# Index scores inside the query tiles, two ranking steps behind every search round, and attention outputs normalised per tile

## The reference, cut to what matters

```
h = rms_norm(x); q, k, v, qi, ki, wi, xp = split(h @ w_in)       # rotary on q, k, qi, ki
prompt:  sc[q, key] = sum_h wi[q, h] * relu(qi[q, h] . ki[key])    # 8 index heads, causal
         sel = top_k(sc, 128);  o = softmax(q.k over sel) @ v      # 8 heads, 2 kv heads
sample:  the same over 2048 cached keys in pages: 256 are selected, their k and v rows gathered
pool:    m = (window mean(xp) - xp) @ w_pool * scale
x = x + rms_norm([o, m] @ w_out)
x = x + rms_norm((gelu(conv(h2 @ w_gate)) * (h2 @ w_val)) @ w_down)
```

## Time and profile before

| what | value |
|---|---|
| three runs | 1585.71, 1589.93 (median), 1590.79 us |
| profiled execution | 1585.85 us, of which the span is 1584.1 us |
| busy in the span | PE 1435.0, weight loads 1239.6, DVE 803.7, ACT 432.3, POOL 184.1 us |
| granted clock over the span | 0.932 of 2.4 GHz |

### The profile page before, as it was taken

How to read it: one execution, slowest core, us unless ns; L and a number is a source line. 1 busy time by engine, 2 the same in 40 slices (tenths; PEclk the granted TensorE clock), 3 DMA queues, 4 the chain that set the end, 5 groups by cost and what they waited for, 6 DMA issues and landing times. The chain is left out here.

```text
span 1584.1 us, 25392 instructions
## 1 busy us (share of the span) xinstructions
PE 1435.0 (91%) x9676; PEld 1239.6 (78%) x9676; DVE 803.7 (51%) x1752; ACT 432.3 (27%) x761; POOL 184.1 (12%) x200
## 2 busy tenths in 40 slices
PE   4999957998899999999988988599979999999995
PEld 2765643687899999999957547356969999999995
DVE  1127777434665656712142486863366565665221
ACT  3111113534322222422131120254342222224220
POOL 1000354002100000000040005430030000000002
PEclk8999976898999999999979999587989999999997
DMA  8870112002122222222159402020212222222321
GB/s 322 176 103 27 34 36 77 5 28 80 67 93 89 85 91 93 86 97 88 69 215 172 87 1 70 1 81 1 80 41 94 93 87 87 91 103 74 111 76 54
DMA packets 46316, 133.17 MB, mean 84 GB/s; under 512 B 6319, under 2 KB 25615, under 8 KB 38911
## 3 DMA queue, kind: packets, MB, share of 16 engines
q1 hardware_dynamic: 43423, 119.52, 25.2%
q0 software_dynamic: 2816, 12.62, 2.3%
HBM read 119.94 MB, written 12.82 MB: 84 GB/s over the span
## 5 line engine op out<-in xcount | busy, mean ns | idle before, releaser
L779 PE MATMUL ps<-moR_r,W_r 128*128 128x260 f32 x1408 | 285.4, 284 | 0.0
L779 PEld LDWEIGHTS ps<-moR_r,W_r 128*128 128x128 f32 x1408 | 218.1, 190 | 0.0
L779 PE MATMUL ps<-hT_r,QZC_r 128*128 128x260 f32 x896 | 183.4, 286 | 0.0
L779 PE MATMUL ps<-moR_r,QZC_r 128*128 128x260 f32 x704 | 146.5, 289 | 12.3 <-DVE hT_r L1822 12.1
L779 PE MATMUL ps<-moR_r,SQ_r 128*128 128x260 f32 x704 | 142.1, 283 | 0.0
L779 PEld LDWEIGHTS ps<-hT_r,QZC_r 128*128 128x128 f32 x896 | 141.3, 193 | 0.0
L779 PE MATMUL ps<-hT_r,SQ_r 128*128 128x260 f32 x704 | 140.6, 281 | 0.0
L766 PE MATMUL ps<-hT,W 128*128 128x260 f32 x576 | 132.8, 388 | 0.0
L779 PEld LDWEIGHTS ps<-moR_r,QZC_r 128*128 128x128 f32 x704 | 110.6, 192 | 16.0 <-issue 8.6
L766 PEld LDWEIGHTS ps<-hT,W 128*128 128x128 f32 x576 | 109.4, 192 | 17.1 <-issue 0.6
L1864 DVE TENSOR_TENSOR SEL<-ps,rstd 128x520 f32<-128x520 f32 x44 | 30.8, 700 | 154.3 <-PE ps L779 149.4
(11 more groups left out here) (318 smaller groups left out, 2728.0 us busy)
## 6 DMA issues: line engine op xcount, KB each, us to landing
W<-in_w_gates SPq DMA_DIRECT2D x44, 512.0 KB, 3.2
W<-in_w_vals SPq DMA_DIRECT2D x44, 512.0 KB, 3.2
W<-in_w_downs SPq DMA_DIRECT2D x16, 1408.0 KB, 6.0
W<-in_w_pairs SPq DMA_DIRECT2D x12, 1024.0 KB, 7.5
pages_by_slot<-moR SPq DMA_DIRECT2D x8, 1024.0 KB, 5.4
yR<-pages_by_slot SPq DMA_DIRECT2D x16, 512.0 KB, 17.9
W<-in_w_outs SPq DMA_DIRECT2D x8, 1024.0 KB, 4.9
W<-in_w_kv SPq DMA_DIRECT2D x2, 1312.0 KB, 10.3
```

Of the source, the lines that this page charges most:

```text
L779: last = mm(ps[:, 2 * (g % 2) + f, 0:HT], w(k), x(k)[:, f * HT:(f + 1) * HT], start=(k == 0 and n == 0), stop=(k == nk - 1 and n == 2))
```

## The change

Dots are taken in the order of head pairs and put into the products of QI_T+2, QI_T+3, XP_T and XP_T+1, six each, behind the steps named in `at`; DVE adds them between its rotary steps. Ranking of tile 1 and the search come after all of them. Each of the 20 search steps is followed by `rank(2)`, the nineteenth by three more, and the rest of the ranking is spread over attention steps 3 to 23. In attention the probabilities are no longer scaled. `values` takes the transposed probabilities as weights (128 columns) and moves 64 columns of v, so that outputs have queries on partitions; per tile DVE scales them at once (`outputs_normed`), PE turns them back in four transposes, ACT copies them. `keys_turned` moves from steps 21 to 24 to steps 17 to 20, `pick_d` from 6 to 5, `pick_e` from 9 to 7, `pool_tiles` from 14 to 24, where its evacuation moves from ACT to DVE.

```diff
-SCORED = 10
-ROPES = {16: (4,), 18: (5,), 19: (6,)}
+DOTS = [(t, h) for j in range(4) for t in (1, 2, 3) for h in (2 * j, 2 * j + 1)]
+ROPES = {12: (4,), 15: (5,), 17: (6,)}
 # PE
+                def dot(d):
+                    def go():
+                        t, h = DOTS[d]
+                        if d == 0:
+                            pe.wait_ge(*kt_ev(l, 4))
+                        if d % 6 == 0:
+                            wait_alone(pe, *rope_done(l, d // 6 + 1))
+                        if d >= 2:
+                            wait_alone(pe, *dot_relu(l, d - 1))
...
-                    tile8(QI_T + j, 1 + j // 2, j % 2)
+                    tile8(QI_T + j, 1 + j // 2, j % 2, extras=dots, at=range(2, KD) if j >= 2 else ())
...
+                steps = [scores_by_page] + [count(s) for s in range(COUNTS)] + [pick_a, pick_b, pick_c]
+                page_products()
+                arrived(l, 4)
+                for j in (2, 3):
+                    pe.wait_ge(*evac(l, XP_T + j - 1))
+                    tile8(XP_T + j, 4, j % 2, extras=steps, at=(1, 4, 7) if j == 2 else (1, 3, 5, 7))
...
-                    wait_alone(pe, *list_ev(l, 1))
-                    pe.wait_ge(*o_ev(l, 1))
+                    wait_alone(pe, *ss_ready(l, 1))
+                    pe.wait_ge(*qs_ev(l, 2))
+                    pe.wait_ge(*o_ev(l, 2))
...
-                picks = {6: pick_d, 14: pool_tiles, 26: sample_scores, 28: scores_by_row, 33: sample_probs_turned,
-                         34: sample_values}
-                picks.update({21 + q: (lambda q=q: keys_turned(q)) for q in range(4)})
+                def outputs_turned(t):
+                    wait_alone(pe, *o_normed(l, t + 1))
+                    for j in range(4):
+                        last = turn(ps[:, 6 + t % 2, j * P:(j + 1) * P], ON[:, j * P:(j + 1) * P], ident)
+                    last.then_inc(o_turned.sem, 1)
+                picks = {5: pick_d, 21: sample_scores, 23: scores_by_row, 24: pool_tiles, 28: sample_probs_turned,
+                         30: sample_values}
+                picks.update({17 + q: (lambda q=q: keys_turned(q)) for q in range(4)})
+                turned = {8 * t + 12: t for t in range(NT - 1)}
...
-                    pe.wait_ge(*prob_ready(l, i + 1))
+                    pe.wait_ge(*exp_done(l, i + 1))
...
-                        last = mm(ps[64 * n:64 * n + 64, 6 + t % 2, j * P:(j + 1) * P],
-                                  NAT[:, kt, 200 + 64 * n:264 + 64 * n], ART[:, i % 2, kt * P:(kt + 1) * P],
+                        last = mm(ps[:, 6 + t % 2, 64 * p:64 * p + 64], ART[:, i % 2, kt * P:(kt + 1) * P],
+                                  NAT[:, kt, 200 + 64 * n:264 + 64 * n], start=(kt == 0), stop=(kt == t))
 # DVE
-                for j in range(4):
-                    rope(j)
+                for ropes, first in (((0,), 0), ((1,), 6), ((2, 3), 12)):
+                    for j in ropes:
+                        rope(j)
+                    for d in range(first, first + 6):
+                        add_dots(d)
...
-                    d = SCORED + 1 + n
-                    if d < 24:
-                        add_dots(d)
-                        rank(1 if d >= 16 else 0)
-                    else:
-                        rank(2)
+                    rank(2)
                     for j in ROPES.get(n, ()):
                         rope(j)
-                rank(4)
-                rope(7)
+                    if n == 18:
+                        rank(3)
+                        rope(7)
...
+                def outputs_normed(t):
+                    dve.wait_ge(*pv_mm(l, N_HEADS * (t + 1)))
+                    if t:
+                        dve.wait_ge(*o_turned(l, t))
+                    nc.vector.reciprocal(sums[:, t % 2, :], sums[:, t % 2, :]).then_inc(o_recip.sem, 1)
...
-                    if 4 <= i < 2 * N_HEADS:
-                        rank(-(-len(ranks) // (2 * N_HEADS - i)))
+                    if 3 <= i < 24:
+                        rank(-(-len(ranks) // (24 - i)))
```

More of the change, by code:

```diff
@@ L416, in build @@
         pms_mm = Signal("pms_mm", 1)
+        pm_ev = Signal("pm_ev", 4)
         pms_ev = Signal("pms_ev", 1)
@@ L758, in arrived, with product @@
                 pe.wait_ge(*w_in_slot[c % 2](l, 16 * dmas_before(c)))
-            def product(g, lhsT, rhs, nk, extras=None, before=None):
+            def product(g, lhsT, rhs, nk, extras=None, at=(), before=None):
                 for k in range(nk):
@@ L821, in partner @@
                     last.then_inc(rot_mm.sem, 1)
+                def dot(d):
[7 more added lines that the diff above has]
+                            wait_alone(pe, *dot_relu(l, d - 1))
+                        rows = slice(64 * (h % 2), 64 * (h % 2) + 64)
+                        mm(ps[:, 4 + d % 2, 0:P * (t + 1)], qiT[rows, h // 2, t * P:(t + 1) * P],
+                           kiT[rows, 0:P * (t + 1)], start=True, stop=True).then_inc(dot_mm.sem, 1)
+                    return go
+                dots = [dot(d) for d in range(24)]
                 for j in range(4):
@@ L844, in layer @@
                 partner(3)
+                arrived(l, 3)
+                pe.wait_ge(*evac(l, XP_T - 1))
+                tile8(XP_T, 3, 0, extras=dots, at=range(2, KD))
                 pe.wait_ge(*rope_done(l, 4))
@@ L850, in layer @@
                 mm(ps[:, 7, 0:8], const("ofrow", 8), WI[0:8, 4, :], start=True, stop=True).then_inc(qib_mm.sem, 1)
-                arrived(l, 3)
-                pe.wait_ge(*evac(l, XP_T - 1))
-                tile8(XP_T, 3, 0)
+                pe.wait_ge(*evac(l, XP_T))
+                tile8(XP_T + 1, 3, 1, extras=dots, at=range(1, KD - 1))
                 pe.wait_ge(*qib_ev(l, 4))
@@ L938, in layer @@
                     pe.wait_ge(*evac(l, Q_T + j - 1))
-                    tile8(Q_T + j, 5 + j // 2, j % 2, extras=counts)
+                    tile8(Q_T + j, 5 + j // 2, j % 2, extras=steps, at=(1, 4, 7))
                     if j >= 1:
@@ L1057, in layer @@
                         picks[i]()
+                    elif steps:
+                        steps.pop(0)()
+                    if i in turned:
+                        outputs_turned(turned[i])
                     if 2 <= i < UNITS + 2:
@@ L1219, in layer, with relu @@
                 copy(kT[:, SEQ:TOK], ps[:, 7, 8:8 + NB]).then_inc(kt_ev.sem, 1)
-                q_copy(2, QI_T + 2)
-                q_copy(3, QI_T + 3)
+                def relu(d):
+                    t, h = DOTS[d]
+                    n = P * (t + 1)
+                    act.wait_ge(*dot_mm(l, d + 1))
+                    if d >= 4:
+                        act.wait_ge(*dot_acc(l, d - 3))
+                    nc.scalar.activation(RB[:, d % 4, 0:n], ps[:, 4 + d % 2, 0:n], ACT.Relu).then_inc(dot_relu.sem, 1)
+                for j in range(2):
+                    for d in range(6 * j, 6 * j + 6):
+                        relu(d)
+                    q_copy(2 + j, QI_T + 2 + j)
+                for d in range(12, 18):
+                    relu(d)
                 def xp_copy(j):
@@ L1281, in exponentials @@
                         act.wait_ge(*pt_mm(l, i - 3))
[L1282 to L1284 removed]
+                    t, p = divmod(i, N_HEADS)
+                    nc.scalar.activation(ARP[i % 4][:, 0:n], ARS[:, i % 2, 0:n], ACT.Exp, bias=att[:, i % 4:i % 4 + 1], scale=-1.0,
+                                         accum_out=sums[:, t % 2, p:p + 1]).then_inc(exp_done.sem, 1)
                 def probs_copied(i):
@@ L1582, in layer @@
                 ts(spread, const("spread"), wcol[:, 8:9], None, ALU.mult).then_inc(w_spread.sem, 2)
+                for d in range(18, 24):
+                    add_dots(d)
                 dve.wait_ge(*sdot_mm(l, 1))
@@ L1587, in layer @@
                 nc.vector.tensor_reduce(snew[:, :], sdot[:, :], AX.X, ALU.add).then_inc(snew_ready.sem, 1)
-                for d in range(8):
-                    add_dots(d)
                 for r in range(TOPK_P // 8):
```

210 lines of the change are left out of this document (90 added, 120 removed).

## The result

The changed kernel takes 1638.16 us (median of 4 runs, 1637.46 to 1641.43) against 1590.36 before: ratio 1.031, 95% interval 1.029 to 1.034. It is slower, as forecast, but by 48 us and not by 26, and 1638 lies 5 us above the range. The profiled execution took 1641.43 us, 55.6 more than that of before.

A forecast was written before the change was run, and what follows sets the result against it. It saw a path through DVE's ranking, search, attention and list, then POOL's gather, then PE. Keys at 1050.4 plus 70.9, less 0.8, made 14 us a layer, 28 in all: 1614, stated as 1616, range 1592 to 1633.

The forecast's parts named there:

- Page products: Dots moved ahead of the page products in layer 1: 17.5 us later, page products at 910.6.
- search: Search behind the ranking of tile 1: starts at 930, takes 72.0 us, rounds of 3.18 set by DVE.
- attention start: Attention starts on DVE at 1002 in place of 990.05, 12 us late.
- list: First attention steps with one-hot rows take 12.2 us; the list is ready at 1021.8, 3 us earlier than before.
- The gather: Keys land at 1050.4, 28.6 us after the list; PE reaches step 17 near 1042 and waits 8 us.
- hidden after all: Rival: PE reaches step 17 later or the list comes 12 us earlier, so no gather wait; 1588, chance 0.10.
- the faster one: Rival: ranking hides in DVE's wait for PE's count during search, saving up to 21 us; 1580, chance 0.07.
- The tail: PE work from the keys at step 17 to the output projection: 60.4 us, plus the slow-clock allowance.
- 10.5 for the slow clock: Tail allowance: 1.5 behind the gather wait, 7 behind the sample scores, 2 behind the sample values.
- the slow clock holds: Rival: PE stays at 0.50 from the keys through the pool tiles, 6 us a layer more; 1626, chance 0.14.
- the 0.8: Taken off the projection's start at 1121.3, as its first matmuls may find the full clock.
- The value matmuls: Turned value matmuls in attention, 64 moving and 128 weight columns: priced by weight load, 0.21 for two passes, no gain.

The follow-up runs named there:

- pool14: The changed kernel with the pool tiles moved back from attention step 24 to step 14: 1647.9 us.
- late_rows: The changed kernel with pool tiles at step 14 and gathered-row work at the old steps (keys 21, sample scores 26, sample values 34): 1604.3 us.
- late_wide: late_rows with most value matmuls moving their 64 columns of v twice (128 columns): 1585.3 us.
- after_wide: The changed kernel with most value matmuls moving their 64 columns of v twice and nothing else: 1626.7 us.
- straight_early: The changed kernel with the old kernel's value matmuls, scaling and output copies, gathered keys still at step 17: 1632.6 us.
- after_dense: The changed kernel plus unread 128 x 512 matmuls, six before the wait for gathered rows and four before the row scores: 1626.1 us.
- late_dense: late_rows plus four unread 128 x 512 matmuls ahead of the row scores: 1611.7 us.
- late_one: late_rows with one ranking action per search round in place of two: 1612.0 us (1597.5 to 1621.1).

## Why the prediction was wrong in size

- **Page products, search, attention start, list** (17.5, 72.0, 12.2): held within 2.5 us. The 2 us come from the dots' stretch (page products 912.7). There the third rotary step cost 1.7 and not 1.0, the wait for the new score 0.65 and not 0.4, and the rotation product at 879.25 ran at the slow clock, 1.86 us to the next row where before had 0.96. The search's 72.0 measured 72.1 (960.18 to 1032.29).
- **The gather:** the wait appeared, in both layers, at the first key transpose, 5.6 for 8, because PE reached step 17 at 1047.3 and not 1042, at the slow clock already. The "hidden after all" rival (0.10) is out, and so is the faster one.
- **The tail, 60.4 and 10.5 for the slow clock: here is the step that failed.** The mechanism was named, the price was wrong. 77.6 was measured in layer 1 and 80.7 in layer 0, so with my 60.4 the clock costs 17.2 and 20.3. I took 10.5 from the old kernel, where the clock returned 13 us after the sample scores, and assumed it would return as soon in the new one. It came back for good only behind the pool tiles. With full-clock steps of 2.48 us in tile 3 (1134.76 to 1137.24) instead of my 2.66, 60.4 was if anything too much, and 17.2 too little. The wait for the rows was priced as a wait. pool14 and late_rows, 44 us apart, show that using the rows early costs far more than the wait's 3 to 6 us, since the clock is down at the keys and stays down.
- **The rival "the slow clock holds" (0.14, 6 a layer)** happened and was too cheap: 6.7 more in the tail of layer 1, and the 0.8 that I had taken off for the projection's first matmuls did not come. PE's slow way to step 17 cost nothing, it only shortened the wait. I had priced the rival for the keys to the pool tiles alone; the 17 us from the sample values to the projection ran at 0.50 too.
- **The value matmuls:** "no gain" was nearly right for their price: four products of tile 3 take 0.94 at the full clock against 1.01 before (1093.63 to 1094.64 in PE's timeline), and 0.99 with 128 moved columns in late_wide (1079.83 to 1080.82). But I weighed only what a product costs at a given clock and not what it does to the clock. late_wide shows that, on the kernel with the late rows: 1604.3 became 1585.3.
- **Behind the projection's start** I had zero; 3.9 and 3.4 us came, from where the clock fell in the feed-forward part. Other kernels of this study scatter as much there with the same instructions, so as far as the runs show this part is luck, bad luck here.
- **The sum** for layer 1 in the profiled execution: keys 2.5, tail 6.7, projection 0.8, behind it 3.4, so 13.4 beyond the forecast of 14. Twice 27.4 is 54.8, and 55.6 was measured.

A product of two passes with 128 weight and 64 moving columns takes 0.235 us here at the full clock and 0.433 at the half one (1.73 for four). The Trainium skill (TensorE: Matmul & The Clock Gate, LDWEIGHTS) gives a weight load as its columns over 1.2 GHz, 0.107 us for 128; the estimate from it for the two passes is 0.21, as in the prediction. The trace agrees at the full clock, within 0.03; at 0.50 it does not, the product takes twice that. So the rule was sound for the sum at the full clock and did not cover the half of the tail that ran at the other.

What stays open: what keeps the clock down between the keys and the pool tiles. The few columns alone don't: neither double columns (after_wide) nor the old value matmuls (straight_early, layer 0) brought it back for good there, while with dense matmuls in the wait it was 1.00 at the keys and fell only at the sample scores (after_dense). Whether the wait or the key transposes do it was not tried apart. Open too is why late_wide itself scatters by 20 us.

## What to carry to other kernels

Before turning a matmul so that it moves fewer columns, look at the granted clock around it: with the late rows the columns were nearly free at the full clock (0.99 against 0.94 us for four products), and without them the clock stayed at 0.50 for some 48 us. Where a profile shows PE busy without a gap at 0.50, try moving columns that nobody reads: it made two kernels faster here, and four dense matmuls in a third gave nothing. And a late transfer costs nothing while PE comes to it later still: moving its consumer forward makes every delay ahead of it visible, and here the clock was down behind that wait. So the halves of such a change are priced together.

## What the runs showed of the hardware that was not expected

- PE busy 85.88 of 87.10 us with the clock at 0.50 throughout (pool14, layer 1), with 64-column value matmuls, transposes and scores.
- Ten more matmuls of 128 x 512 a layer made that kernel 36 us faster; 128 in place of 64 moved columns made another one 19 us faster, at a price of 0.05 us per four products at the full clock.
- The clock was full behind the pool tiles and behind the added dense matmuls each time (after, pool14, late_dense), but in late_dense it was lost again within 12 to 16 us, and in pool14 within 12.
- The same program can differ by 24 us from one execution to the next (late_one, 1597.48 at a clock of 0.914, 1621.09 at 0.897), and its two layers by 15.6 us from the first index-query tile to the projection in one execution, where the two of the kernel before differ by 1.9.
